# A two-layer diffusion step on one core: modulation chunks loaded ahead of the first weights, row norms one at a time, gathers one step ahead

## What is computed

```
for l in range(DEPTH):
    sh1, sc1, g1, sh2, sc2, g2 = split(silu(cond) @ w_ada[l] + b_ada[l], 6)
    h   = rms_norm(x, norm1_g[l]) * (1 + sc1) + sh1
    z   = h @ w_in[l]                    # 4 mixer branches + 4 gates
    mix = (sum over n of sigmoid(gate_n) * (branch_n @ w_branch[l, n])) @ w_out[l]
    x   = x + g1 * mix
    h   = rms_norm(x, norm2_g[l]) * (1 + sc2) + sh2
    aff = softmax(h @ w_router[l]); g, idx = top_k(aff.T, cap)    # 16 experts choose rows
    a, u = h[idx] @ w_gate, h[idx] @ w_up
    x   = x + g2 * scatter_add(idx, ((silu(a) * u) @ w_down) * g)
y = rms_norm(x, final_norm_g)
```

## Time and profile before

| | us |
|---|---|
| median of 3 runs | 1724.0 (1723.58 to 1724.09) |
| the profiled execution's own time | 1723.84 |
| its span in the profile | 1721.7 |
| PE busy in the span | 1570.8 (91%), mean granted clock 0.993 |
| DVE, ACT, POOL busy | 540.9, 448.7, 326.5 |
| DMA queue q1 | 535.43 MB, 75.9% of 16 engines |

### The profile page before, as it was taken

One profiled execution on the slowest core, in us unless ns is written; L12 is line 12 of the kernel. 1 busy time (PEld: TensorE's weight loads), 2 busy tenths in 40 slices (PEclk: granted clock), 3 DMA queues, 4 the chain that ended last, 5 costly groups with the idle time before them and its releaser, 6 DMA issues.

```text
span 1721.7 us, 20678 instructions
## 1 busy us (share of the span) xinstructions
PE 1570.8 (91%) x8261; PEld 937.5 (54%) x8261; DVE 540.9 (31%) x896; ACT 448.7 (26%) x822; POOL 326.5 (19%) x184
## 2 busy tenths in 40 slices
PE   4999999999999989899889999999999998998986
PEld 2988889944334333243269888997533432432422
DVE  2634454423221221121158245443332221222123
ACT  3435554213112011020043455531220111200201
POOL 1564455500000000000035545553000000000000
PEclk8999999999999999999999999999999999999999
DMA  8723534367999999999994433346499999999995
GB/s 351 254 98 112 191 147 147 149 291 292 409 428 429 427 428 428 428 427 428 423 360 154 144 148 147 147 160 258 180 408 426 427 427 427 428 426 429 427 427 222
DMA packets 52068, 536.28 MB, mean 311 GB/s; under 512 B 13584, under 2 KB 13992, under 8 KB 20264
## 3 DMA queue, kind: packets, MB, share of 16 engines
q1 hardware_dynamic: 52008, 535.43, 75.9%
HBM read 533.05 MB, written 2.36 MB: 311 GB/s over the span
## 4 chain that ended last, share of the span: by engine, by line
PE 69%; DMA 20%; DVE 4%; ACT 4%; issue 2%; SPq 0%; DVEq 0%; ACTq 0%
PE psum L913 22%; PE psum L1680 18%; DMA ring<-in_w_e_down 10%; PE psum L1709 8%; DMA ring<-in_w_e_gu 7%; PE psum L1146 4%; PE psum L1076 3%; DMA ring<-in_w_ada 3%; PE psum L1647 3%; PE psum L1726 2%; PE psum L685 2%; DVE arena L1844 1%; PE psum L1049 1%; PE psum L1028 1%; DVE arena L1854 1%
## 5 line engine op out<-in xcount | busy, mean ns | idle before, releaser
L913 PE MATMUL psum<-HTH,WSR 128*128 128x384 f32 x1536 | 412.7, 342 | 4.1 <-DVE HTL L1355 3.9
L1680 PE MATMUL psum<-ring,arena 128*64 128x512 f32 x1536 | 341.9, 595 | 27.1 <-DMA ring<-in_w_e_gu 27.1
L913 PEld LDWEIGHTS psum<-HTH,WSR 128*128 128x128 f32 x1536 | 280.4, 188 | 17.6 <-issue 11.4
L859 POOL TENSOR_TENSOR WSR<-ring,WSR 128x1024 fp32r<-128x1024 f32 x96 | 233.6, 2434 | 267.2 <-ACT WSR L1165 267.2
L913 PE MATMUL psum<-HTL,WSR 128*128 128x384 f32 x768 | 259.4, 338 | 0.0
L1680 PEld LDWEIGHTS psum<-ring,arena 128*64 128x64 f32 x1536 | 106.5, 137 | 247.7 <-issue 196.7
L1854 DVE TENSOR_TENSOR arena<-arena,psum 64x512 f32<-64x512 f32 x64 | 44.1, 690 | 469.3 <-ACT arena L1763 469.3
L1763 ACT ACTIVATE arena<-psum 64x512 f32<-64x512 f32 x64 | 37.7, 589 | 563.1 <-PE psum L1680 562.4
L1165 ACT ACTIVATE WSR<-ring 128x1024 fp32r<-128x1024 f32 x96 | 101.6, 1059 | 291.4 <-PE psum L913 290.0
L1709 PE MATMUL psum<-ring,arena 128*64 128x512 f32 x768 | 172.8, 596 | 3.6 <-DMA ring<-in_w_e_down 3.6
L1844 DVE TENSOR_TENSOR arena<-psum,GROW 32x512 f32<-32x512 f32 x128 | 87.9, 687 | 210.1 <-PE psum L1709 208.8
(11 more groups left out here) (214 smaller groups left out, 1533.6 us busy)
## 6 DMA issues: line engine op xcount, KB each, us to landing
ring<-in_w_e_gu SPq DMA_DIRECT2D x96, 2048.0 KB, 26.4
ring<-in_w_e_down SPq DMA_DIRECT2D x48, 2048.0 KB, 29.4
ring<-in_w_ada SPq DMA_DIRECT2D x24, 2048.0 KB, 9.2
ring<-in_w_in SPq DMA_DIRECT2D x24, 2048.0 KB, 8.1
arena<-in_w_e_gu SPq DMA_DIRECT2D x16, 2048.0 KB, 28.5
arena<-in_w_e_gu SPq DMA_DIRECT2D x16, 1536.0 KB, 22.5
arena<-in_w_e_down SPq DMA_DIRECT2D x8, 2048.0 KB, 23.6
arena<-in_w_e_down SPq DMA_DIRECT2D x8, 1536.0 KB, 26.2
```

The lines of the kernel that those rows point to most:

```text
L859: nc.gpsimd.tensor_tensor(WSR[:, 1, i % 2], part_src(i), WSR[:, 0, i % 2].bitcast(F32), ALU.subtract).then_inc(S["w_rest"], 1)
L913: ins = nc.tensor.matmul(ps[:, 0:TOK], WSR[:, w, i % 2, k, :], x[:, k, :], start=(k == 0 and w == 0 and x is HTH), stop=(k == KT - 1 and w ...
L1680: ins = nc.tensor.matmul(pb[half][64 * m:64 * m + 64, :], XE[:, k, j, :], w[:, half * CH:(half + 1) * CH], start=(k == 0), stop=(k == KT - 1))
```

## The change

1. The opening loads: chunks 1 and 3 go ahead of `w0` in both layers, and `w0` is loaded as two halves of 1 MB with a semaphore each. On the host the words of `w0` are put in the order of the halves; the first half holds parts 0 and 1, the second parts 2 and 3.
2. The high part of part 0 is made after the copies of chunks 1 and 3, and its rest is subtracted by DVE, not by POOL.
3. Idle products on PE in layer 0's opening: nine before chunk 0, three before chunk 2, two each before chunks 1 and 3.
4. Row norms one tile at a time, in the order 1, 2, 0: square, root (with the mean and the epsilon inside the ACT instruction), reciprocal, scaled row. The combination at a group's end takes the same order.
5. In the experts ACT copies the prompt half of each result (two instructions of 32x512), DVE scales only the sample half (two instead of four). The prompt's gate is applied after the combination, by one more DVE instruction per half.
6. Gathers: two, not three, ahead of the first step, then one per step, the last two together in step 5. Two idle products instead of three at the group's end.
7. SP waits for the first gain before it loads the gate rows, since these now serve as scratch.

The diff, cut to its core; unchanged lines are indented less than in the file:

```diff
-      E.add(f"y{j}", 4 + j % 2)
+      E.add(f"y{j}", 4 + j % 2, 2)
   for i in range(6):
       E.add(f"cm{i}", i)
+  COMBINED = [(t, half) for t in (1, 2, 0) for half in range(2)]
...
   def opening_pe(pe, layer):
 
       for i, c in enumerate((0, 2)):
+          if i and layer == 0:
+              idle_products(5, 3)
           pe.wait_ge(once[f"ada_in{c}"], layer * 16 + 16)
...
-  def row_squares(act, layer, t):
+  ROWS = (1, 2, 0)
+
+  def row_norm(act, layer, i):
+
+      t = ROWS[i]
       nc.scalar.activation(XN[:, t, :], X[:, t, :], ACT.Square, accum_out=SS[:, t:t + 1]).then_inc(S["op_sq"], 1)
-
-  def row_roots(act, layer):
-      act.wait_ge(S["op_ms"], stood(layer, "op_ms") + 1)
-      nc.scalar.activation(SD[:, 0:TT], MS[:, 0:TT], ACT.Sqrt).then_inc(S["op_sd"], 1)
-
-  def row_scales(dve, layer):
-      dve.wait_ge(S["op_sq"], stood(layer, "op_sq") + TT)
-      nc.vector.tensor_scalar(MS[:, 0:TT], SS[:, 0:TT], 1.0 / D, EPS, ALU.mult, ALU.add).then_inc(S["op_ms"], 1)
-      dve.wait_ge(S["op_sd"], stood(layer, "op_sd") + 1)
-      nc.vector.reciprocal(RS[:, 0:TT], SD[:, 0:TT]).then_inc(S["op_rs"], 1)
+      act.wait_ge(S["op_sq"], stood(layer, "op_sq") + i + 1)
+      nc.scalar.activation(SD[:, t:t + 1], SS[:, t:t + 1], ACT.Sqrt, scale=1.0 / D, bias=MS[:, 3:4]).then_inc(S["op_sd"], 1)
+
+  def row_scale(dve, layer, i):
+
+      t = ROWS[i]
+      dve.wait_ge(S["op_sd"], stood(layer, "op_sd") + i + 1)
+      nc.vector.reciprocal(RS[:, t:t + 1], SD[:, t:t + 1]).then_inc(S["op_rs"], 1)
 
   def scaled_rows_dve(dve, layer):
-      dve.wait_ge(S["op_rs"], stood(layer, "op_rs") + 1)
-      for t in (1, 2):
-          nc.vector.tensor_scalar(XN[:, t, :], X[:, t, :], RS[:, t:t + 1], None, ALU.mult).then_inc(S["op_xn"], 1)
-
-  def scaled_rows_act(act, layer):
-      act.wait_ge(S["op_rs"], stood(layer, "op_rs") + 1)
-      nc.scalar.activation(XN[:, 0, :], X[:, 0, :], ACT.Identity, scale=RS[:, 0:1]).then_inc(S["op_xn"], 1)
+
+      for i in range(TT):
+          row_scale(dve, layer, i)
+          if i < TT - 1:
+              dve.wait_ge(S["op_rs"], stood(layer, "op_rs") + i + 1)
+              t = ROWS[i]
+              nc.vector.tensor_scalar(XN[:, t, :], X[:, t, :], RS[:, t:t + 1], None, ALU.mult).then_inc(S["op_xn"], 1)
+
+  def scaled_row_act(act, layer):
+
+      t = ROWS[-1]
+      act.wait_ge(S["op_rs"], stood(layer, "op_rs") + TT)
+      nc.scalar.activation(XN[:, t, :], X[:, t, :], ACT.Identity, scale=RS[:, t:t + 1]).then_inc(S["op_xn"], 1)
...
   def load_first_weights(eng, layer):
 
-      eng.dma_start(ring[:, unit_at["w0"][0], :], w_unit(layer, "w0")).then_inc(once["w_in0"], 16)
+      for half in range(2):
+          words = slice(half * KT * 2 * P, (half + 1) * KT * 2 * P)
+          eng.dma_start(ring[:, unit_at["w0"][0], words], w_unit(layer, "w0")[:, words]).then_inc(once[f"w_in0_{half}"], 16)
...
-      load_first_weights(sp, 0)
       for c in (1, 3):
           load_ada(sp, 0, c)
+      load_first_weights(sp, 0)
...
+      idle_products(5, 9)
       opening_pe(pe, 0)
...
-          pool.wait_ge(S["w_high"], base("w_high") + i + 1)
-          nc.gpsimd.tensor_tensor(WSR[:, 1, i % 2], part_src(i), WSR[:, 0, i % 2].bitcast(F32),
-                                  ALU.subtract).then_inc(S["w_rest"], 1)
+          if i == 1:
+              pool.wait_ge(S["w_rest"], base("w_rest") + 1)
+          if i:
+              pool.wait_ge(S["w_high"], base("w_high") + i + 1)
+              nc.gpsimd.tensor_tensor(WSR[:, 1, i % 2], part_src(i), WSR[:, 0, i % 2].bitcast(F32),
+                                      ALU.subtract).then_inc(S["w_rest"], 1)
...
               for c in (1, 3):
+                  if l == 0:
+                      idle_products(5, 2)
                   ada_main(pe, l, c)
...
       for k in range(0, KT, 2):
           if k == 0:
-              w_high(0)
               act.wait_ge(S["op_gain"], base("op_gain") + 1)
           elif k == 4:
               for c in (1, 3):
                   copy_out(f"ada{c}", adas(c), lambda ps: ps)
+              w_high(0)
               act.wait_ge(S["sc_ready"], base("sc_ready") + 1)
...
               gain(0, 1, 48, 1)
+              dve.wait_ge(S["w_high"], base("w_high") + 1)
+              nc.vector.tensor_tensor(WSR[:, 1, 0], part_src(0), WSR[:, 0, 0].bitcast(F32), ALU.subtract).then_inc(S["w_rest"], 1)
               dve.wait_ge(S["sc_ready"], base("sc_ready") + 1)
...
-          for name in ("ada0", "ada2", "w0", "ada1", "ada3"):
+          for name in ("ada0", "ada2", "ada1", "ada3", "w0"):
...
-          for k in range(3):
+          for k in range(2):
...
-                  if j == 0 and k % 2 == 0 and k and 0 in halves:
-                      gather(k + 1)
-                      if k + 2 < KT:
-                          gather(k + 2)
-                      else:
+                  if j == 0 and 0 in halves and 0 < k < KT - 1:
+                      for ahead in ((k + 1,) if k < KT - 3 else (k + 1, k + 2) if k == KT - 3 else ()):
+                          gather(ahead)
+                      if k == KT - 2:
                           affinities_t()
...
-          idle_products(E.at["xe0"][0], 3)
+          idle_products(E.at["xe0"][0], 2)
           e_copied(pe, g, "pg")
           e_copied(pe, g, f"y{GRP-2}")
           e_copied(pe, g, f"y{GRP-1}")
-          for i, (t, half) in enumerate((t, h) for t in range(TT) for h in range(2)):
+          for i, (t, half) in enumerate(COMBINED):
...
               at_copy(j)
-
-      for t in range(TT):
-          if t == TT - 1:
-              nc.scalar.activation(SD[:, 3:4], RS[:, 0:1], ACT.Sqrt)
-          act.wait_ge(S["x_done"], base("x_done") + (NE // GRP - 1) * TT + t + 1)
-          row_squares(act, l + 1, t)
-      row_roots(act, l + 1)
+              ps = e_take(act, g, f"y{j}")
+              for half in range(2):
+                  ins = nc.scalar.activation(YP[32 * j:32 * j + 32, half * CH:(half + 1) * CH],
+                                             ps[64 * half + 32:64 * half + 64, :], ACT.Copy)
+              e_release(ins, f"y{j}")
+
+      nc.scalar.activation(SD[:, 3:4], MS[:, 3:4], ACT.Sqrt)
+      for i in range(TT):
+          act.wait_ge(S["x_done"], base("x_done") + (NE // GRP - 1) * TT + i + 1)
+          row_norm(act, l + 1, i)
       if l < DEPTH - 1:
           opening_copies(act, l + 1)
...
-                  for dst, i, lo in ((YS, 1, 64 * half), (YP, 0, 64 * half + 32)):
-                      ins = nc.vector.tensor_tensor(dst[rows, cols], ps[lo:lo + 32, :], GROW[lo:lo + 32, 1, i, cols], ALU.mult)
+                  ins = nc.vector.tensor_tensor(YS[rows, cols], ps[64 * half:64 * half + 32, :],
+                                                GROW[64 * half:64 * half + 32, 1, 1, cols], ALU.mult)
               e_release(ins, f"y{j}")
...
-              e_release(nc.vector.tensor_tensor(X[:, t, cols], X[:, t, cols], ps, ALU.add), f"cm{i}")
+              if t:
+                  e_release(nc.vector.tensor_tensor(X[:, t, cols], X[:, t, cols], ps, ALU.add), f"cm{i}")
+              else:
+                  nc.vector.tensor_tensor(GROW[:, 0, 1, cols], ps, GROW[:, 1, 0, cols], ALU.mult).then_inc(S["prompt_part"], 1)
+                  dve.wait_ge(S["prompt_part"], base("prompt_part") + 2 * g + half + 1)
+                  e_release(nc.vector.tensor_tensor(X[:, t, cols], X[:, t, cols], GROW[:, 0, 1, cols], ALU.add), f"cm{i}")
...
-      row_scales(dve, l + 1)
       if l < DEPTH - 1:
           scaled_rows_dve(dve, l + 1)
           opening_gains(dve, l + 1)
       if l > DEPTH - 2:
-          dve.wait_ge(S["op_rs"], stood(l + 1, "op_rs") + 1)
           dve.wait_ge(once["fin_g_in"], 16)
-          for t in range(TT):
+          for i, t in enumerate(ROWS):
+              row_scale(dve, l + 1, i)
+              dve.wait_ge(S["op_rs"], stood(l + 1, "op_rs") + i + 1)

```

39 lines of the change are left out of this document (21 added, 18 removed).

## The result

The changed kernel takes **1714.33 us** (median of 4 runs, 1711.71 to 1717.64) against 1724.05 before (1723.58 to 1724.94): a ratio of 0.9944, 95% interval 0.9925 to 0.9963, so 0.56% faster. A second measurement of it, among the experiments, gave 1716.88 (7 runs, 1715.39 to 1719.85; ratio 0.9959, 0.9945 to 0.9973). Both lie in the forecast's range. The runs of the two lie 5.9 and 4.5 us apart, which was not foreseen; the kernel before, 1.4 us apart in its four runs here, spreads by 3.4 to 7.5 us in the 10 to 17 runs beside the experiments. Three executions far outside the others (1921.17, 2341.16 and 4376.88 us) are left out of all medians and ranges. This table cuts the profiled spans at the same seven events of PE's timeline; "goes on" is where PE leaves its stand within the first tile of a layer's input product.

What follows compares the result with a forecast made beforehand. Experts were taken as bound by DMA transfers, mixers by PE's own chain. Gains of 3.1 + 1.8 + 2.8 + 2.0 = 9.7 us off the profiled 1723.84 gave 1714.1, as a median 1714.2; range 1709.8 to 1718.9.

Steps and rivals of the forecast that it cites:

- Opening of layer 0: Layer 0's start: loading `w0` last brings PE's products forward 3.5 us, less 0.4 for DVE beside POOL: 3.1 us net.
- chunk 3 is there by then: Layer 0's opening, full-clock case: chunk 3 has landed by 30.8 us, when chunk 1's product ends.
- the three clocks: Layer 0's opening: half clock throughout (1.2 us later), full from 27.4 (5.2 earlier), or full from about 30.8 (3.5 earlier).
- full clock from about 30.8: Layer 0's opening, the case chosen: clock rises during chunk 1's product, second product ends at 35.9, 3.5 us earlier.
- the case that I gave less weight: Layer 0's opening: full clock from 27.4 us on, second product ends at 34.2, 5.2 us earlier.
- The 0.4 us for DVE beside POOL: Both openings: a cast now meets POOL's subtraction and runs after it, delaying the last rest by an estimated 0.4 us.
- Fall of the clock after 49 us: Layer 0's opening: up to 1.7 us more gain if the half-clock spell after 49 us is gone.
- Gathers: First expert group of each layer: PE's 0.90 us wait before the selection transposes goes, refill earlier: 0.9 per layer, 1.8.
- Opening of layer 1: Layer 1's start: chunk 1's product starts earlier, chunk 3 has just landed; 3.2 us less 0.4: 2.8 us gain.
- End: Kernel's end: row norms of tiles 1 and 2 are ready earlier, scaled rows end at 1716.4 instead of 1718.5: 2.0 us.
- the rival with full clock throughout: Layer 0's opening: clock stays full, no spell at 49; 6.5 us gained instead of 3.1, total 1710.8; chance 0.17.
- The rival on the other side: Layer 0's opening: idle products never bring the clock up; 9.2 + 0.4 lost, 6.6 won, total 1727.0; chance 0.03.

Runs made afterwards that it cites:

- run 8: The changed kernel once more, no edit, for the spread of its runs and a second profile: 1716.88 us, ratio 0.9959.
- run 7: Changed kernel without layer 0's idle products, POOL's part 1 waiting for DVE's last rest, old gathers with selection transposes two steps earlier in another bank: 1712.62 us.
- run 1: Changed kernel without the idle products of layer 0's opening: 1713.60 us, ratio 0.9943.
- run 6: Changed kernel with all four instructions on a split result on DVE again, ACT copying none: 1718.54 us, ratio 0.9973.
- run 4: Changed kernel with the rest of part 0 on POOL again; load order and ACT's late high part stay: 1716.76 us, ratio 0.9959.
- run 9: Changed kernel with the rest of part 1 on DVE too, behind its last rest of the input; POOL begins with part 2: 1709.67 us, ratio 0.9918.
- run 10: Changed kernel with part 1's rest on DVE and without the idle products of layer 0's opening: 1709.24 us, ratio 0.9917.
- run 12: Kernel before with the new load order, ACT's later high part of part 0, and part 0's rest on DVE: 1718.93 us, ratio 0.9968.
- run 11: Kernel before with the new load order alone and ACT's high part of part 0 at its new place: 1722.23 us, ratio 0.9991.
- run 5: Changed kernel where POOL takes up part 1's rest only when DVE has its last rest of the input: 1715.38 us, ratio 0.9951.

## Why the prediction was right, and where not

- **Opening of layer 0, 3.1 forecast, 4.3 and 5.4 measured.** The load order does what was said, with one limit: in the first profile both products stand on PE's chain, but where the clock stays up chunk 3's load binds again, for 0.64 us until 31.69 in the second profile ("chunk 3 is there by then", at 30.8, was too early). The step that failed is the choice among the three clocks, "full clock from about 30.8". In the first profile it was back by 29, within the idle pair, in the second it didn't fall; the ends, 34.62 and 33.61, surround the 34.2 of the case that I gave less weight. The fall is not fixed from run to run (0.52 and 1.00 in 28 to 29 us). The Trainium skill, page "TensorE: Matmul & The Clock Gate", section "What's actually happening", says that the number of slow products at a kernel's start differs between runs of one kernel; these profiles agree (the nine idle products at the start take 8.94 and 7.94 us).
- **The 0.4 us for DVE beside POOL.** From the end of the second product to PE's going on it was 9.19 us and is 9.59 and 9.57: the size was right. The way was another: the cast still came in 0.03 us ahead of POOL; POOL's own second rest had grown to 1.34 from about 1.0 and pushed POOL's part 1, and with it the last rest, back by that.
- **Fall of the clock after 49 us, "up to 1.7 more".** Gone in the first profile (1.6 won to the first gather), back in the second (that stage 1.1 longer than before). It should have been a term with two outcomes in each layer; its size, 1.7 us, was right (1.7 and 1.6 in run 8).
- **Gathers, 1.8 forecast, 0 measured.** The wait of 0.90 went, but the refill came only 0.3 us earlier behind the first gather: a step is now a gather and eight products, 2.73 us (start 408.74 to 411.48), two steps were 5.12 (417.28 to 422.40), so each costs 0.17 more; and the pair of steps 4 and 5 is freed 1.5 us later. Even the full microsecond of run 7 moved nothing that shows. Two steps failed: the wait of 0.90 was taken over whole into the refill's time, and an earlier refill was taken to shorten the stream. The likely reason, argued and not shown, is how were read: 334 GB/s were taken for a queue that runs empty, but the DMA engines' busy share in the same row is 0.94, which leaves 0.3 us in five.
- **Opening of layer 1, 2.8 forecast, 2.2 and 2.3 measured.** The gain's 1.6 us came, chunk 3 was there, and the products follow each other. Where the clock stays up during them (run 1: 3.64 us for both) PE goes on 28.6 us behind the last product, 3.4 less than before; the two profiles of the changed kernel had it at half, which the sum had no term for. Chunk 3, forecast to have "just landed", doesn't set the pace: in runs 1 and 6 the products are released by ACT's tile, and run 6, which starts the combination 1.6 us later, loses 1.4 of it at the same clock.
- **End, 2.0 forecast, 2.3 measured.** The combination starts 1.57 us earlier behind the last product (1.4 forecast), the prompt tile's extra work takes 1.2 of it back, and the three scaled rows follow the last add, which is worth 1.8. Ten profiles with these pieces have 16.5 to 16.6 us there; run 6, without the split of the results, has 18.1.

So 1714.2 against 1714.33 is partly luck: up to the first gather of layer 0 the first profile had won 6.0 us (411.00 to 405.05) where 3.1 were forecast, near the 6.5 of the rival with full clock throughout, and the gathers' 1.8 fell out on the other side; the repeat lies 2.6 higher. What carries the change is the load order, and only together with what lets the first tile start after it: order alone 1.6 us, not clear of noise, with part 0's rest on DVE 4.5, with the halves and the rest of the change 7 to 10. By run 4 the rest's engine makes no difference in the median once the other pieces are there, though layer 1 of its profile is 1.8 us later. The rival on the other side, idle products that never bring the clock up, fell with the first rows above: nine in 8.94 us, and chunk 0's product behind them at 1.92.

## What to carry to other kernels

A load order pays only if the next thing in line is ready too: moving the modulation chunks ahead made the first weights the late ones, and loading them as one block, with a slow subtraction behind it, gave nearly all of the gain back. Before a rate below its peak is read as an empty queue, look at the busy share beside it: here it was 0.94, and a refill up to 1 us earlier won nothing that shows. Before a stage is compared between two profiles, look at the granted clock in both: half clock in one of them hid a loss of 1.4 us (run 6). And where two engines meet on a shared resource, move the work off the pair rather than only later; the wait that was merely delayed stood at the next tile.

## What the runs showed of the hardware

- The granted clock falls to half also behind stands of PE of no more than 2.1 us, in some executions and not in others: behind the stand of layer 0 in the second profile of the changed kernel and not in the first, where the kernel is the same. Such a fall put PE 1.7 and 1.6 us back (layers 0 and 1 of that profile). With shorter stands (0.43 us, runs 9 and 10) no fall followed them in either layer, and the five runs each lie within 2.6 and 1.7 us of each other. That the falls make the spread isn't shown: runs 4 and 12, which keep stands of 1 to 3 us, have 2.6 too, and the kernel before spreads by 3.4 us and more beside the experiments. In the profiles the first loads also come in at different times: chunk 2's product starts at 18.84 us in run 11 and at 20.88 in the kernel before.
- POOL's 128x1024 subtraction beside DVE makes a 0.56 us instruction take 2.60, and 0.17 take 1.96, and leaves a cast that came first alone. The Trainium skill, page "SBUF — State Buffer", section "Who interferes with whom", says that an instruction of DVE with both inputs in SBUF contends with one of POOL that reads SBUF; the rows agree, and run 5, where the meeting is gone, has 0.56.
- From the first gather to the last product of a layer the experts take 448 to 451 us in all profiles, also where the queue was refilled up to 1 us sooner.
